# Fewer adaLN pieces at the output projection and the router, more inside the mixer and in attention's softmax loop

## The chip, the cores and the metric

One Trainium2 chip, one core of it. The metric is the device time of one launch in microseconds (us), lower is better. TensorE is called PE here, VectorE DVE, ScalarE ACT, GpSimd POOL and SyncE SP; SP issues nearly all transfers.

## The reference, cut to what matters

Two networks run one behind the other on 256 tokens of width 1024. The first has two layers, each a mixer and then sixteen experts:

```python
for layer in range(DEPTH):            # DEPTH = 2
    h = h + hybrid_mixer(rms_norm(h, norm1_g[layer]), w_in[layer], ..., w_out[layer], lb)
    h = h + expert_choice_ffn(rms_norm(h, norm2_g[layer]), w_router[layer], w_gate[layer],
                              w_up[layer], w_down[layer])
```

The second network has two layers too: pooling with an MLP, then attention with an MLP. Each modulates its inputs with six vectors, which come from a small conditioning vector through a large matrix, for the latent rows (`c`) and the context rows (`c_ctx`):

```python
sh1, sc1, gt1, sh2, sc2, gt2 = split(silu(c) @ w_ada[i] + b_ada[i])     # w_ada[i]: 1024 x 6144
h_lat = modulate(rms_norm_2(x, g_mix_pre[i]), sh1, sc1)
x = x + gt1 * rms_norm_2(mixer(h_lat), g_mix_post[i])
x = x + gt2 * rms_norm_2(mlp(modulate(rms_norm_2(x, g_mlp_pre[i]), sh2, sc2)), g_mlp_post[i])
```

All of it is float32. The 24 pieces `w_ada[i][:, 512 n : 512 n + 512]` depend on nothing else in the computation, so each may be loaded and multiplied wherever the kernel has room before its vector is wanted. A piece is written (layer, n) below; (1, 10) and (1, 11) make `gt2` of the second layer, wanted only by the last MLP.

## The kernel before, in words

The work is laid out by hand, one program for each engine. All weights pass through a ring of slots of 2 MB: seven fixed ones, and up to four more while the experts run (two in `ring_extra`, one each in `ring_late` and `ring_early`), which lie in memory that the mixer uses until its last matmuls. `items` gives every load its slot and its place in one order of use. The counter `weights_used` rises by one for each used item; a load waits until it has passed the value stored in `free_at`. SP issues loads strictly in the order of its own program, so a load whose slot isn't free holds back all behind it.

**A mixer** (layers 0 and 1 of the first network) runs nine projections. The last four (RV, HI, RG, HG) go by rows: for each of two row tiles t, `project_rows` does 24 matmuls (L567 to L569, three for each of eight chunks, since each product is split into high and low parts), then `one_level` does one level of a scan (L723; DVE prepares it). Behind some of these eight steps, those in `EARLY_AFTER`, `early_ada` puts one ada piece: first the columns of the piece before (`ada_columns`, L595), then the product (`ada_item`, L580), whose row ACT copies out (`ada_row`). All early pieces share one ring slot, called d, so each is loaded only when the one before has been used. Behind them come the scan's outputs (`hgrn_out`, L753 and L755). SP waits for these before it loads anything into `ring_extra`.

**Output projection and router.** `rest_ada(0)` and `rest_ada(1)` lie between the parts of the output projection (`w_out`), `rest_ada(2)` before the second tile's logits, and `rest_ada(3)` behind the turned affinities, all in slots b and d. Then tokens are gathered (L902) and the experts begin; SP loads their weights as slots come free.

**Attention** takes 16 steps u (`scores` L1399, softmax on DVE and ACT, `turn_probs` L1408, `values` L1420 every second step), then the product with `w_o` (L1449). Two more pieces follow it. `ADA_LAST` names the pieces that are done in the second network; their slot is ring slot 6. POOL makes a diagonal of `gt2` and PE turns it into rows (`post_rows`, L1201).

Of the kernel before, what the change touches and what calls it, by code (L numbers as in the profile page):

```python
# [87 lines left out]

EARLY_AFTER = ((RV, 0), (RV, 1), (HI, 1), (RG, 0), (HG, 0), (HG, 1))


def pieces(layer, first, end):
    return [(layer, n) for n in range(first, end)]


ADA_EARLY = (pieces(0, 0, 6), pieces(0, 10, 12) + pieces(1, 0, 4))
ADA_REST = (pieces(0, 6, 10), pieces(1, 4, 6) + pieces(1, 10, 12))
ADA_LAST = pieces(1, 8, 10) + pieces(1, 6, 8)  # L100


GROUP = 4
# [21 lines left out]
def build_program(nc, x, cols, w_in, w_out, w_router, w_gate, w_up, w_down, final_g, ctx_x, w_ada,  # L125
# [221 lines left out]
    for layer in range(DEPTH):  # L347
        rounded_free.append(count[2][4:6])
        a, b, c, d = sorted(range(4), key=lambda slot: count[2][slot])
        early = iter(ADA_EARLY[layer])  # L350
        for n, kind in enumerate(PROJECTIONS):
            if (kind, 0) in EARLY_AFTER:
                item(("ada", *next(early)), d, 1)
            item(("mix", layer, n), (a, b, c, d, a, b, c, a, b)[n], 1)
            if (kind, 1) in EARLY_AFTER:
                item(("ada", *next(early)), d, 1)
        for piece, slot in zip(ADA_REST[layer], (b, d)):
            item(("ada", *piece), slot, 1)
        rounded = [4 + (SPLITS * layer + j) % 2 for j in (OUT_0, OUT_1)]
        own = RING1 - 1  # L360
        for n in range(2):
            item(("w_out", layer, n), (c, a)[n], 1)
            count[2][rounded[n]] = count[0]
        for piece, slot in zip(ADA_REST[layer][2:], (b, d)):
            item(("ada", *piece), slot, 1)
        slots = itertools.chain((rounded[0], c, RING1, RING1 + 1, own, EARLY, a, b, d, rounded[1],
                                 LATE),
                                itertools.cycle((c, rounded[0], own, a, b, d, rounded[1])))
        for e in range(NEXP):
            for n in (0, 2):  # L370
                for part, slot in enumerate(sorted(itertools.islice(slots, 2))):
                    item(("moe", layer, e, n + part), slot, 2 if (e, n) == (0, 0) else 1)
            for n in (4, 5):
                item(("moe", layer, e, n), next(slots), 1)
            if e in CTX_MID[layer]:
                item(("ctx", CTX_MID[layer][e]), next(slots), 1)
# [6 lines left out]
    ring2, last_pieces = itertools.cycle(order2), [("ada", *piece) for piece in ADA_LAST]  # L383
    for layer in range(DEPTH):
        item(last_pieces[layer], RING1 - 1 if layer else next(ring2), 1)
        for name in block2_first(layer):
            item(name, next(ring2), 1)
        if layer:
            item(last_pieces[2], RING1 - 1, 1)
            item(last_pieces[3], next(ring2), 1)  # L390
        for n in range(16):
            item(("mlp", layer, n), next(ring2), 1)
# [136 lines left out]
    def _(pe):  # L529
# [73 lines left out]
        for l in range(DEPTH):  # L603
# [172 lines left out]
            def rest_ada(k):  # L776
                ada_item(ADA_REST[l][k], 2)

# [52 lines left out]
            def logits(t):  # L831
# [6 lines left out]
                for c in range(KC):  # L838
# [7 lines left out]
            out_0 = len(PROJECTIONS)  # L846
            rows_times(take(pe, names[0], 0), 0, out_0, 1, chunks=first)
            turn_mixed(1, lambda t: freed(pe, ("hgrn_o", l, t)))
            rest_ada(0)
            rows_times(take(pe, names[1], 1), 1, out_0, None, chunks=first)  # L850
            fill(rows_times(psum[0], 0, out_0, 1, chunks=second), names[0])
            rest_columns(0)
            rest_ada(1)
            fill_and_release(rows_times(psum[1], 1, out_0, None, chunks=second), names[1],
                             ("w_out", l, 0))
            rest_columns(1)
            for t in range(NT):
                name = ("w_out", l, 1, t)
                ins = rows_times(take(pe, name, t), t, out_0 + 1, None, amid if t else {})
# [3 lines left out]
                    fill(ins, name)  # L863

            turn_rows(1)
            rest_ada(2)
            logits(1)
            rest_columns(2)
            pe.wait_ge(S_("affinity_ready"), NT * (l + 1))
            name = ("affT", l)  # L870
            ps = take(pe, name, 5)
            for t in range(NT):
                ins = turn(ps[0:NEXP, t * P:(t + 1) * P], aff[:, t, :], ident)
            fill(ins, name)
            rest_ada(3)
            rest_columns(3)

            def spread_out(part):

# [508 lines left out]

        for pair in range(2):
            turn_queries(pair, 2 + pair)  # L1390
        for pair in range(2):
            freed(pe, ("qT", pair))
        freed(pe, "kT")
# [31 lines left out]
        for u in range(NQ * NT):  # L1425
            if u == 1:
                for pair in (2, 3):
                    turn_queries(pair, 2 + pair)
            if u + 2 == NQ:
                for pair in (2, 3):  # L1430
                    freed(pe, ("qT", pair))
            if u + 2 < NQ * NT:
                scores(u + 2)
            if u and u % 2 == 0:
                values(u // 2 - 1)
            turn_probs(u)
        values(NQ - 1)
        freed(pe, ("o", NQ - 4))
        freed(pe, ("o", NQ - 3))
# [26 lines left out]
    def _(act):  # L1466
# [89 lines left out]
        for l in range(DEPTH):  # L1556
# [102 lines left out]
                  scale=1.0 / W4).then_inc(S_("std_ready"), 1)  # L1659
            high_item(l, OUT_1)  # L1660
            high_chunks(("mix", l), mix_gain, (2, 3))
            for k in range(2):
                ada_row(ADA_REST[l][k])


            def out_ready(t):
                for n in range(2):
# [15 lines left out]
                           lambda _, t=t: xs[:, t, :], first=t)  # L1683
                odd_rows(t)
            step(f(spare[:, :], eps[:, :], ACT.Exp))
            ada_row(ADA_REST[l][2])
            for t in range(NT):
                expect("router_max_ready")
                name = ("logit", l, t)
                ps = full(act, name)  # L1690
                free(f(logit[:, t, :], ps[:, 0:NEXP], ACT.Exp, scale=rinv[:, t:t + 1],
                       bias=rstats[:, t, 1:2], accum_out=rstats[:, t, 2:3]), name)
            ada_row(ADA_REST[l][3])

            def ctx_stats(src):

# [258 lines left out]

        for pair in range(2):
            query_copies(pair)

        def exponentials(u):
            expect("score_max_ready")  # L1960
# [6 lines left out]
        for u in range(NQ * NT):  # L1967
            if u + 1 < NQ * NT:
                exponentials(u + 1)
            if u == 1:  # L1970
                for pair in (2, 3):
                    query_copies(pair)
            name = ("pT", u)
            ps = full(act, name)
            t = u % NT
            free(f(prT[:, :, t * P:(t + 1) * P], ps[:, :].rearrange("p (a t) -> p a t", a=4),
                   ACT.Copy), name)
        first_high(1)
        for t in range(NT):
            bank_stats(t, [("wo", n, t) for n in range(2)])  # L1980
# [13 lines left out]
    def _(dve):  # L1994
# [110 lines left out]
        for l in range(DEPTH):  # L2105
# [267 lines left out]
                    free(tt(h[:, t, part], h[:, t, part], ps[:, :], ALU.add), name)  # L2373

            gains(l, 0, "g_mix_pre")
            ada_bias(("rest", l), ADA_REST[l])
            if l == 0:
                gains(0, 1, "g_mlp_pre")

            def ctx_normalise():  # L2380
# [369 lines left out]
        score_max(0)  # L2750
        score_max(1)
        gains(1, 1, "g_mlp_pre")
        for u in range(NQ * NT):
            freed(dve, ("s", u))
            step(reciprocal(soft[:, u % 4, 3:4], soft[:, u % 4, 2:3]))
            ts(pr[:, u % 2, :], pr[:, u % 2, :], soft[:, u % 4, 3:4], None,
               ALU.mult).then_inc(S_("prob_ready"), 1)
            if u + 2 < NQ * NT:
                score_max(u + 2)
            if u >= 2 and u % 2 == 0:  # L2760
                take_values(u // 2 - 1)
        take_values(NQ - 1)
        first_low(1)
        for t in range(NT):
# [14 lines left out]
    def _(pool):  # L2779
# [62 lines left out]
        diagonal(0, 1, 0, "g_mlp_post")  # L2842
        split_odd_banks("xm0")
        clear_sums(NT, X4_BEFORE["mlp0"])
        freed(pool, ("rest", 1))
        full(pool, ("rows_mlp0", 0, 1))
        diagonal(1, 0, 0, "g_mix_post")
        full(pool, ("rows_mix1", 0, 1))
        diagonal(1, 1, 0, "g_mlp_post")
        split_odd_banks("xm1")  # L2850
        clear_sums(NT, X4_BEFORE["mlp1"])
# [3 lines left out]
    def _(sp):  # L2855
# [20 lines left out]
        for l in range(DEPTH):  # L2876
# [30 lines left out]
            def load_expert(e, n):  # L2907
# [5 lines left out]
                else:  # L2913
# [3 lines left out]

            names = ([("mix", l, n) for n in range(len(PROJECTIONS))] + [("moe", l, FIRST_OWN)]
                     + [("w_out", l, n) for n in range(2)] 
                     + [("ada", *piece) for piece in ADA_EARLY[l] + ADA_REST[l][0:2]])  # L2920
            def turn_of(name):

                name = ("moe", l, 0, name[2]) if name[0] == "moe" else name
# [47 lines left out]
            for e in range(NEXP):  # L2971
                for n in (2, 3, 0, 1, 4, 5) if e == 0 else range(6):
                    if (e, n) == (1, 2):
                        full(sp, ("logit", l, NT - 1))
                        load_expert(1, 4)
                    if (e, n) == (2, 1):
                        ctx_rows_and_bands()
                    if (e, n) not in ((0, FIRST_OWN), (0, 5), (1, 3), (1, 4)):
                        load_expert(e, n)
                    if (e, n) == (0, 3):  # L2980
                        freed(sp, ("hgrn_o", l, NT - 1))
                        sp.dma_start(wr[:, :, :], w_router[l].rearrange("(p c) e -> p c e", c=KC)
                                     ).then_inc(S_("router_landed"), 16)
                        load_expert(0, 5)
                        for piece in ADA_REST[l][2:]:
                            early(("ada", *piece))
                    if (e, n) == (0, 1):
                        load_expert(1, 3)
                if e in CTX_MID[l]:
                    load_ctx(CTX_MID[l][e])  # L2990
        for l in range(DEPTH):
# [10 lines left out]
                else:  # L3002
                    load(name, chunked(w_o[:, (n - 3) * 512:(n - 2) * 512]), eight)

            names = block2_first(l) + (last_pieces[1:] if l else last_pieces[:1])
            if l == 0:
                sp.wait_ge(S_("ctx_x_ready"), 2 * NT)
                full(sp, (("cxa", 1), 3))
# [13 lines left out]
                             src.rearrange("(c p) n -> p c n", p=P)).then_inc(landed[slot], 16)  # L3022

            for n in range(4):
                sp.wait_ge(weights_used, free_at[("mlp", l, n)])
                mlp_load(n, w_mlp_in[l, :, n % 2 * 512:(n % 2 + 1) * 512],
                         w_mlp_out[l, n % 2 * 512:(n % 2 + 1) * 512, :])
# [111 lines left out]
```

## Time and profile before

| | |
|---|---|
| median of 3 runs | 1953.57 us (1952.56 to 1953.98) |
| the profiled execution | 1954.41 us, its span in the profile 1952.6 us |
| busy: PE / DVE / ACT / POOL | 87% / 41% / 27% / 2% of the span |
| moved | 626.57 MB, 321 GB/s on average |
| chain that ended last | PE 58%, DMA 32%, ACT 4%, DVE 4% |

The stages, from the profile's slices and windows: mixer 0 to about 168 us; output projection, router and experts of layer 0 to about 700 us; mixer 1 to about 872 us; the experts of layer 1 to about 1406 us; pooling and the first MLP to about 1629 us; attention to about 1755 us; the last MLP to the end. From 60 to 168 us the 16 DMA engines are busy 0.63 of the time and PE 104.92 of 108 us. In the table of windows below, the DMA share can read slightly over 1, since busy times are rounded for each packet. A duration on PE holds the tail of the pipeline, so the distance from one row's start to the next is what an operation takes from PE's time.

### The profile page before, as it was taken

The page shows a single profiled execution, that of the slowest core. Times are in us where ns is not written, and L with a number is a line of the kernel's source. Part 1 is how long each engine was busy: PE and PEld are TensorE (multiplying, and loading weights), DVE is VectorE, ACT ScalarE, POOL GpSimd, SP SyncE. Part 2 cuts the span into 40 slices and gives each one's busy share as a digit, 9 for nine tenths or more (in the row PEclk, how much of TensorE's full clock was granted, in tenths as well). Part 3 has the DMA queues.
Part 4 walks back from the last instruction along what each step waited for, and adds up shares of the span by engine and source line. Part 5 has one row for each costly group of instructions (what it writes and reads, how often), then busy time and mean ns, then how long its engine had stood idle before and what let it go on. Part 6 is the DMA issues. An engine that isn't in the chain of part 4 may idle for free.

```text
span 1952.6 us, 26219 instructions
## 1 busy us (share of the span) xinstructions
PE 1696.5 (87%) x10892; PEld 1125.2 (58%) x10892; DVE 791.1 (41%) x1203; ACT 526.9 (27%) x802; POOL 30.0 (2%) x27
## 2 busy tenths in 40 slices
PE   7999877689888679998868887977789999999998
PEld 6877433245344249776343543522279985448897
DVE  6595312101111044975101111120077676647776
ACT  5633222100000037342100000021164343444342
POOL 0000000000000000000000000000030000000000
PEclk9999889889989989998989989979799999999999
DMA  9478999999999995679999999999955464315451
GB/s 358 162 269 335 425 430 421 427 422 423 420 427 421 426 385 182 242 265 419 427 423 423 423 424 421 426 428 423 416 190 196 172 233 154 129 49 208 175 182 55
DMA packets 125511, 626.57 MB, mean 321 GB/s; under 512 B 5091, under 2 KB 7779, under 8 KB 100198
## 3 DMA queue, kind: packets, MB, share of 16 engines
q1 hardware_dynamic: 124978, 624.85, 79.5%
q8 instruction: 73, 1.20, 0.2%
q10 hardware_dynamic: 436, 0.32, 0.1%
q14 instruction: 24, 0.20, 0.0%
HBM read 622.01 MB, written 3.15 MB: 320 GB/s over the span
## 4 chain that ended last, share of the span: by engine, by line
PE 58%; DMA 32%; ACT 4%; DVE 4%; issue 1%; SPq 0%; POOL 0%; DVEq 0%; ACTq 0%
DMA ring<-in_w_up 15%; PE bank L567 9%; PE bank L569 9%; PE bank L568 9%; DMA ring<-in_w_mlp_in 8%; DMA ring<-in_w_mlp_out 6%; PE bank L1086 6%; PE bank L1104 5%; PE bank L947 5%; PE bank L1332 2%; PE bank L580 2%; PE bank L1449 1%; DMA ring<-in_w_down 1%; PE bank L982 1%; PE bank L723 1%; DMA ring<-in_w_ada 1%
## 5 line engine op out<-in xcount | busy, mean ns | idle before, releaser
L947 PE MATMUL bank<-ring,xeT 128*32 128x512 f32 x1920 | 266.4, 702 | 98.2 <-DMA ring<-in_w_up 97.8
L947 PEld LDWEIGHTS bank<-ring,xeT 128*32 128x32 f32 x1920 | 68.6, 121 | 283.5 <-issue 283.0
L475 ACT ACTIVATE silu_g<-bank 128x256 f32<-128x256 f32 x32 | 12.3, 383 | 690.1 <-PE bank L947 690.1
L475 DVE TENSOR_TENSOR hid_e<-silu_g,bank 128x256 f32<-128x256 f32 x32 | 13.5, 421 | 374.0 <-ACT silu_g L475 374.0
L2567 DVE TENSOR_TENSOR w_low<-ring,w_high 128x1024 fp32r<-128x1024 f32 x128 | 152.4, 1233 | 10.2 <-ACT w_high L1858 5.3
L1858 ACT ACTIVATE w_high<-ring 128x1024 fp32r<-128x1024 f32 x128 | 126.5, 1050 | 85.0 <-PE bank L569 85.0
L1086 PE MATMUL bank<-ctx_xT,ring 128*128 128x256 f32 x512 | 125.3, 410 | 26.1 <-DMA ring<-in_w_mlp_in 26.1
L567 PE MATMUL bank<-x_high,w_high 128*128 128x256 f32 x512 | 145.1, 283 | 3.0 <-DVE x_low L475 2.4
L982 PE MATMUL bank<-ring,hid_T 128*32 128x256 f32 x1920 | 120.5, 397 | 30.9 <-DMA ring<-in_w_down 23.6
L568 PE MATMUL bank<-x_low,w_high 128*128 128x256 f32 x512 | 144.8, 283 | 0.0
L569 PE MATMUL bank<-x_high,w_low 128*128 128x256 f32 x512 | 144.7, 283 | 0.0
L1104 PE MATMUL bank<-ring,ctx_hid 128*128 128x512 f32 x256 | 126.1, 655 | 21.2 <-DMA ring<-in_w_mlp_out 21.2
L1086 PEld LDWEIGHTS bank<-ctx_xT,ring 128*128 128x128 f32 x512 | 105.6, 208 | 46.9 <-DMA ring<-in_w_mlp_in 30.4
L567 PE MATMUL bank<-w_high,xs_high 128*128 128x512 f32 x256 | 105.0, 410 | 5.8 <-DVE xT_low L475 4.9
L475 DVE TENSOR_TENSOR w_low<-ring,w_high 128x2048 fp32r<-128x2048 f32 x44 | 100.9, 2293 | 18.8 <-ACT w_high L475 14.6
L1104 PEld LDWEIGHTS bank<-ring,ctx_hid 128*128 128x128 f32 x256 | 53.2, 211 | 92.1 <-issue 66.2
L982 PEld LDWEIGHTS bank<-ring,hid_T 128*32 128x32 f32 x1920 | 59.3, 112 | 81.5 <-DMA ring<-in_w_down 32.6
L569 PE MATMUL bank<-w_high,xT_low 128*128 128x512 f32 x256 | 102.3, 400 | 0.0
L568 PE MATMUL bank<-w_low,xs_high 128*128 128x512 f32 x256 | 102.2, 399 | 0.0
L567 PE MATMUL bank<-w_high,hid_high 128*128 128x512 f32 x256 | 101.0, 395 | 0.0
L569 PE MATMUL bank<-w_high,hid_low 128*128 128x512 f32 x256 | 101.0, 394 | 0.0
L568 PE MATMUL bank<-w_low,hid_high 128*128 128x512 f32 x256 | 100.9, 394 | 0.0
(282 smaller groups left out, 2595.9 us busy)
## 6 DMA issues: line engine op xcount, KB each, us to landing
ring<-in_w_down SPq DMA_DIRECT2D x60, 2048.0 KB, 30.2
ring<-in_w_up SPq DMA_DIRECT2D x60, 2048.0 KB, 24.3
ring<-in_w_gate SPq DMA_DIRECT2D x60, 2048.0 KB, 21.8
ring<-in_w_ada SPq DMA_DIRECT2D x24, 2048.0 KB, 9.6
ring<-in_w_mlp_in SPq DMA_DIRECT2D x24, 2048.0 KB, 8.4
ring<-in_w_mlp_out SPq DMA_DIRECT2D x24, 2048.0 KB, 7.9
ring<-in_w_in SPq DMA_DIRECT2D x16, 2048.0 KB, 9.2
ring<-in_w_out SPq DMA_DIRECT2D x4, 2048.0 KB, 7.8
```

The source lines that it names most:

```text
L475: self.ins, self.mine = op(*args, **kw), "none"
L567: mm(ps, lh, rh, start=first, stop=False, skip_group_check=True)
L568: mm(ps, lh, rl, start=False, stop=False, skip_group_check=True)
L569: return mm(ps, ll, rh, start=False, stop=last, skip_group_check=True)
L580: ins = mm(ps[32 * g:32 * g + 32, :], cT[:, 2 * g + k, :], w[:, 2 * g + k, :], start=k == 0, stop=k == 1)
L947: ins = mm(ps[32 * j:32 * j + 32, :], xeT[:, g % 2, c, i * CAP:(i + 1) * CAP], w[:, :, k, j, :, :], start=c == 0, stop=c == KC - 1, skip_g ...
L982: ins = mm(banks[q // 2][rows_, at_:at_ + 256], hidT[:, j, 32 * block:32 * block + 32], w[:, c, 256 * q:256 * (q + 1)], start=(n, c) == (0 ...
L1086: ins = mm(ps[:, (j % 2) * S:(j % 2 + 1) * S], w[:, c, j * P:(j + 1) * P], cxT[:, c, :], start=c == 0, stop=c == KC - 1)
L1104: ins = mm(ps[:, :], chid[:, c, t * P:(t + 1) * P], w[:, c, half * 512:(half + 1) * 512], start=c == 0, stop=c == 3)
L1332: ins = mm(ps[:, :], xT2[:, c, t * P:(t + 1) * P], w[:, c, :], start=c == 0, stop=c == KC - 1)
L1858: raw(w_high[:, n % 2, quarter(q)], ring[:, slot, quarter(q)], ACT.Copy).then_inc(S_("w_high_ready"), 1)
L2567: nc.vector.tensor_tensor(w_low[:, slot, quarter(q)], ring[:, slot, quarter(q)], w_high[:, n % 2, quarter(q)].bitcast(F32), ALU.subtract). ...
```

## The change

Two of layer 0's ada pieces, (0, 6) and (0, 7), and two that ran in layer 1, (1, 4) and (1, 5), move from between the parts of the output projection into the mixer's two free steps, behind (HI, 0) and (RG, 1). Each mixer has eight early pieces then, one behind every step. Layer 0 keeps two pieces around its router. Layer 1 keeps none there: its (1, 10) and (1, 11) move to attention, where the first is multiplied behind the turning of the first queries and the second between the last two `turn_probs`. Their rows become columns in the first step and behind the last one.

```diff
-EARLY_AFTER = ((RV, 0), (RV, 1), (HI, 1), (RG, 0), (HG, 0), (HG, 1))
+EARLY_AFTER = tuple((kind, t) for kind in (RV, HI, RG, HG) for t in range(2))
...
-ADA_EARLY = (pieces(0, 0, 6), pieces(0, 10, 12) + pieces(1, 0, 4))
-ADA_REST = (pieces(0, 6, 10), pieces(1, 4, 6) + pieces(1, 10, 12))
-ADA_LAST = pieces(1, 8, 10) + pieces(1, 6, 8)
+ADA_EARLY = (pieces(0, 0, 8), pieces(0, 10, 12) + pieces(1, 0, 6))
+ADA_REST = (pieces(0, 8, 10), [])
+ADA_LAST = pieces(1, 8, 10) + pieces(1, 6, 8) + pieces(1, 10, 12)
...
             turn_mixed(1, lambda t: freed(pe, ("hgrn_o", l, t)))
-            rest_ada(0)
             rows_times(take(pe, names[1], 1), 1, out_0, None, chunks=first)
             fill(rows_times(psum[0], 0, out_0, 1, chunks=second), names[0])
-            rest_columns(0)
-            rest_ada(1)
             fill_and_release(rows_times(psum[1], 1, out_0, None, chunks=second), names[1],
                              ("w_out", l, 0))
-            rest_columns(1)
...
             turn_rows(1)
-            rest_ada(2)
+            if ADA_REST[l]:
+                rest_ada(0)
             logits(1)
...
         for pair in range(2):
             turn_queries(pair, 2 + pair)
+        ada_item(ADA_LAST[4], 6)
...
             if u + 2 < NQ * NT:
                 scores(u + 2)
+            if u == 0:
+                last_columns(4, 7)
             if u and u % 2 == 0:
                 values(u // 2 - 1)
             turn_probs(u)
+            if u == NQ * NT - 2:
+                ada_item(ADA_LAST[5], 0)
+        last_columns(5, 1)
         values(NQ - 1)
```

ACT gets the two `ada_row` copies at the same places, and DVE `last_bias(4)` ahead of the loop and `last_bias(5)` behind it. POOL waits for both before the diagonal for the last MLP, where it waited for layer 1's rest before. SP loads both pieces into slot 6, and the piece (1, 6) of `ADA_LAST`, which needs the same slot, behind them, between the first two loads of the last MLP.

## Rows read from the trace of the kernel before

**Rows 1.** Windows: length, busy us of each engine, granted clock, DMA share, GB/s

```profile
168.00:690.00 522.00, 420.35 (x2911) 221.09 (x2910) 89.50 (x161) 57.49 (x106) 2.10 (x2) 0.91 1.01 424
872.00:1400.00 528.00, 427.58 (x2906) 219.90 (x2910) 89.66 (x162) 63.75 (x117) 4.20 (x4) 0.91 1.01 424
```

**Rows 2.** Timeline of PE and one DVE row in the mixers: start, length, operation

```profile
97.57 1.95 PE L723 MATMUL bank<-qdec,kdec 128*128 128x128 f32 x16
99.35 0.95 PE L595 MATMUL bank<-consts_sb,ada_rows 128*128 128x2 f32 x8
100.24 1.92 PE L580 MATMUL bank<-ring,silu_c 128*32 128x512 f32 x16
102.09 0.50 PE L567 MATMUL bank<-w_high,xs_high 128*128 128x512 f32 x1
...
107.77 1.95 PE L723 MATMUL bank<-qdec_even,kdec 128*128 128x128 f32 x16
...
129.28 1.92 PE L580 MATMUL bank<-ring,silu_c 128*32 128x512 f32 x16 [1.22 <-DMA ring<-in_w_ada]
...
832.71 1.93 PE L580 MATMUL bank<-ring,silu_c 128*32 128x512 f32 x16 [1.64 <-DMA ring<-in_w_ada]
...
101.99 1.23 DVE L475 TENSOR_TENSOR qdec_even<-hgrn_q,hgrn_f 128x1024 f32<-128x1024 f32 x1
```

**Rows 3.** Timeline of SP: issues in mixer 0 and at its end

```profile
97.76 0.37 SPq L2865 DMA_DIRECT2D ring<-in_w_in  x1
102.22 0.37 SPq L2865 DMA_DIRECT2D ring<-in_w_ada  x1
...
168.05 0.34 SPq L2865 DMA_DIRECT2D ring_extra<-in_w_gate  x1
```

**Rows 4.** DMA issues, mixers: us to landing of those at 102.22, 131, 805.23

```profile
ring<-in_w_ada SPq DMA_DIRECT2D x1, 2048.0 KB, 9.7
...
ring<-in_w_ada SPq DMA_DIRECT2D x1, 2048.0 KB, 7.9
...
ring<-in_w_ada SPq DMA_DIRECT2D x1, 2048.0 KB, 9.9
```

**Rows 5.** DMA issues, the same columns: those at 168.05, 871.52, 903.94, 929.09

```profile
ring_extra<-in_w_gate SPq DMA_DIRECT2D x1, 2048.0 KB, 9.8
...
ring_extra<-in_w_gate SPq DMA_DIRECT2D x1, 2048.0 KB, 9.2
...
ring<-in_w_up SPq DMA_DIRECT2D x1, 2048.0 KB, 12.3
...
ring<-in_w_down SPq DMA_DIRECT2D x1, 2048.0 KB, 11.7
```

**Rows 6.** Timeline of layer 1's router: PE, and two issues of SP

```profile
903.94 0.33 SPq L2865 DMA_DIRECT2D ring<-in_w_up  x1
...
907.95 1.93 PE L839 MATMUL bank<-router_sb,xT 128*128 128x16 f32 x16 [0.25 <-issue]
...
929.09 0.33 SPq L2865 DMA_DIRECT2D ring<-in_w_down  x1
```

**Rows 7.** Timeline of attention's loop, its first and last steps

```profile
1681.00 4.51 PE L1399 MATMUL bank<-kT,qT 128*128 128x512 f32 x6 [2.29 <-ACT qT L475]
...
1685.21 0.37 DVE L475 SCALAR_TENSOR_TENSOR mod_gain<-mods,cols_sb 128x8 f32<-128x8 f32 x2
...
1685.69 0.16 DVE L475 RECIPROCAL softmax_stat<-softmax_stat 128x1 f32<-128x1 f32 x1
...
1720.87 0.60 PE L1408 MATMUL bank<-consts_sb,prob 128*128 128x128 f32 x4
...
1722.34 0.66 PE L1408 MATMUL bank<-consts_sb,prob 128*128 128x128 f32 x4 [0.87 <-DVE prob L475]
...
1723.73 1.10 PE L1420 MATMUL bank<-probT,kv 128*128 128x256 f32 x4 [0.73 <-issue]
```

**Rows 8.** The diagonal for the last MLP: POOL makes it, PE needs it

```profile
1636.72 1.90 POOL L475 TENSOR_TENSOR diag<-consts_sb,gate_col 128x1024 f32<-128x1024 f32 x1
...
1739.26 1.88 PE L1201 MATMUL bank<-diag,ones 128*128 128x512 f32 x4
```

More of the change, by code:

```diff
@@ L356, in build_program @@
                 item(("ada", *next(early)), d, 1)
-        for piece, slot in zip(ADA_REST[layer], (b, d)):
-            item(("ada", *piece), slot, 1)
         rounded = [4 + (SPLITS * layer + j) % 2 for j in (OUT_0, OUT_1)]
@@ L363, in build_program @@
             count[2][rounded[n]] = count[0]
-        for piece, slot in zip(ADA_REST[layer][2:], (b, d)):
+        for piece, slot in zip(ADA_REST[layer], (b, d)):
             item(("ada", *piece), slot, 1)
@@ L385, in build_program @@
         item(last_pieces[layer], RING1 - 1 if layer else next(ring2), 1)
-        for name in block2_first(layer):
+        for k, name in enumerate(block2_first(layer)):
+            if k == 3:
+                item(last_pieces[4], RING1 - 1, 1)
+                item(last_pieces[5], RING1 - 1, 1)
             item(name, next(ring2), 1)
@@ L865, in _ @@
             turn_rows(1)
-            rest_ada(2)
+            if ADA_REST[l]:
+                rest_ada(0)
             logits(1)
-            rest_columns(2)
+            if ADA_REST[l]:
+                rest_columns(0)
             pe.wait_ge(S_("affinity_ready"), NT * (l + 1))
@@ L874, in _ @@
             fill(ins, name)
-            rest_ada(3)
-            rest_columns(3)
+            if ADA_REST[l]:
+                rest_ada(1)
+                rest_columns(1)
             def spread_out(part):
@@ L1661, in _ @@
             high_chunks(("mix", l), mix_gain, (2, 3))
-            for k in range(2):
-                ada_row(ADA_REST[l][k])
             def out_ready(t):
@@ L1685, in _ @@
             step(f(spare[:, :], eps[:, :], ACT.Exp))
-            ada_row(ADA_REST[l][2])
+            if ADA_REST[l]:
+                ada_row(ADA_REST[l][0])
             for t in range(NT):
@@ L1692, in _ @@
                        bias=rstats[:, t, 1:2], accum_out=rstats[:, t, 2:3]), name)
-            ada_row(ADA_REST[l][3])
+            if ADA_REST[l]:
+                ada_row(ADA_REST[l][1])
             def ctx_stats(src):
@@ L1957, in _ @@
             query_copies(pair)
+        ada_row(ADA_LAST[4])
         def exponentials(u):
@@ L1977, in _ @@
                    ACT.Copy), name)
+            if u == NQ * NT - 2:
+                ada_row(ADA_LAST[5])
         first_high(1)
@@ L2375, in _ @@
             gains(l, 0, "g_mix_pre")
-            ada_bias(("rest", l), ADA_REST[l])
             if l == 0:
+                ada_bias(("rest", l), ADA_REST[l])
                 gains(0, 1, "g_mlp_pre")
@@ L2752, in _ @@
         gains(1, 1, "g_mlp_pre")
+        last_bias(4)
         for u in range(NQ * NT):
@@ L2761, in _ @@
                 take_values(u // 2 - 1)
+        last_bias(5)
         take_values(NQ - 1)
@@ L2844, in _ @@
         clear_sums(NT, X4_BEFORE["mlp0"])
-        freed(pool, ("rest", 1))
         full(pool, ("rows_mlp0", 0, 1))
@@ L2848, in _ @@
         full(pool, ("rows_mix1", 0, 1))
+        freed(pool, ("last", 4))
+        freed(pool, ("last", 5))
         diagonal(1, 1, 0, "g_mlp_post")
@@ L2919, in _ @@
                      + [("w_out", l, n) for n in range(2)]
-                     + [("ada", *piece) for piece in ADA_EARLY[l] + ADA_REST[l][0:2]])
+                     + [("ada", *piece) for piece in ADA_EARLY[l]])
             def turn_of(name):
@@ L2984, in _ @@
                         load_expert(0, 5)
-                        for piece in ADA_REST[l][2:]:
+                        for piece in ADA_REST[l]:
                             early(("ada", *piece))
@@ L3003, in block2_load @@
                     load(name, chunked(w_o[:, (n - 3) * 512:(n - 2) * 512]), eight)
-            names = block2_first(l) + (last_pieces[1:] if l else last_pieces[:1])
+            names = block2_first(l) + (last_pieces[1:2] + last_pieces[3:] if l else last_pieces[:1])
             if l == 0:
@@ L3024, in _ @@
             for n in range(4):
+                if (l, n) == (1, 1):
+                    block2_load(last_pieces[2])
                 sp.wait_ge(weights_used, free_at[("mlp", l, n)])
```

## The prediction, made before the changed kernel was run

> **What bounds the kernel now.** I read the chain that ended last, then the stages in windows, then the timelines of PE and SP around each edit, and last the time that single loads take to land. In both stages of experts the DMA engines are busy all the time at 424 GB/s, while PE is busy for about 0.8 of it [rows 1]. There only two things count: when this stream of loads starts, and how many bytes are in it. The stream starts when the mixer's last matmuls free `ring_extra` [rows 3]. So the end of the mixer on PE sets the start of the next five hundred microseconds. Inside the mixer PE runs without a gap: level, columns, ada product and projection follow each other start to start [rows 2]. DVE had the level that starts on PE at 107.77 ready at 103.22 (101.99 plus 1.23), so it isn't what PE waits for. The only gaps in these steps are those where an ada load is late, 1.22 us in mixer 0 and 1.64 us in mixer 1.
>
> **Work added to the mixers.** A step takes from PE, start to start: level 1.78 (97.57 to 99.35), columns 0.89 (to 100.24), ada product 1.85 (to 102.09), projection 5.68 (to 107.77). A piece more costs 1.85 + 0.89 = 2.7 us, two pieces 5.5 us in each mixer, on the path. The copies of their rows on ACT lie beside PE's next projection.
>
> **Loads that come late.** All eight pieces share slot d. A piece is issued 0.13 us after the one before was used (102.22 against 102.09 [rows 2, 3]) and is wanted one projection, one level and one set of columns later: 5.68 + 1.78 + 0.89 = 8.35, less 0.13, which leaves 8.2 us. Alone, a load lands after 7.9 us, in time by 0.3. Behind another load, issued 4.46 us earlier (97.76 and 102.22), it lands after 9.7 us in mixer 0 and 9.9 us in mixer 1 [rows 4], 1.5 and 1.7 us too late. A projection's weights are issued behind every second row tile, so every second early piece has such a companion. Before, most pieces had a free step ahead of them in which the load could land; the one without it is the 1.22 and 1.64 us gap. After the change two further pieces stand so: the one behind (HI, 0), whose load is the very one issued at 102.22, and the one behind (HG, 0). I take 1.5 + 1.3 us in mixer 0 and 1.7 + 1.6 us in mixer 1. Those behind (HI, 1) and (RG, 1) load alone and cost nothing, at most 1.2 each if they collide after all. The one behind (HG, 1) has the retention output ahead of it. The mixers end later by x = 5.5 + 2.8 = 8.3 us and 5.5 + 3.3 = 8.8 us; with no late load x would be 5.5.
>
> A rule to weigh here. The Trainium skill (DMA: Bandwidth & Descriptors, Anatomy of one DMA) fits a transfer, issued from GpSimd, as about 2.0 us fixed plus its bytes at 436 GB/s. By that estimate a piece of 2 MB lands after 6.8 us, and one that follows a companion by 4.46 us after 7.2 us, so no load would be late and the first rival below would hold. The trace has 7.9 and 9.7 us, from SP [rows 4].
>
> **What layer 0 makes of it.** Before, the DMA engines were still moving the two pieces for the output projection when `ring_extra` came free: its first load took 9.8 us to land [rows 5]. After, these two went earlier, the engines stand idle, and that load takes the 7.9 us of a lone one. Its issue is 8.3 us later, its landing 8.3 - 1.9 = 6.4 us. The stream behind it holds the same bytes as before. The output projection gives PE its 5.5 us back, but that is no help: PE is then 2.8 us late in front of a stream that is 6.4 us late. The two pieces left at this router sit where they sat. Layer 0: +6.4 us. Bounds: +3.6 with no late load, +8.8 if two more loads are late.
>
> **What layer 1 makes of it.** Here two pieces leave the stream, 4.2 MB at 424 GB/s, 9.9 us. Its start is later by 8.8 - 1.3 = 7.5 (the first load took 9.2 [rows 5]), so by bytes alone the stream would end 2.4 us earlier. But loads also need free slots. With the pieces out of the output projection PE ends it 8.8 - 5.5 = 3.3 us late; the load that this frees, at 903.94, landed 12.3 us after its issue and can do it in 7.9: 3.3 - 4.4 = -1.1 us. Then every slot is full until the first expert's first matmuls; the load that they free at 929.09 landed after 11.7 us, at best 7.9: 3.3 - 3.8 = -0.5 us [rows 5, 6]. The latest of the three rules: -0.5 us. The stream is shorter by nearly 10 us, but it runs dry in front of the router and hardly gains. Taking the pieces out of the router's waits gives nothing: the logits start 0.25 us after PE was free [rows 6], held by ACT's and DVE's copies, and PE idles behind them. A gain of up to 0.5 us from ACT's missing copies is possible.
>
> **What attention makes of it.** The first product (1.85 us) fits into the 2.29 us in which PE waits for ACT's copies of the queries [rows 7]. Its columns come behind the scores of step 2, which end at 1685.51, and DVE's bias waits for them in front of the first reciprocal, at 1685.69. Last case: 1685.51 + 0.89, then the bias, about 0.2: 1.0 us late. Best case: the filled gap makes scores end sooner, and only the bias counts, 0.2. I take 0.6. The second product starts at 1721.47 and ends at 1723.3, where the last `turn_probs` started at 1722.34: 1.0 us late. The columns then take 0.89 us of a gap of 0.73 that the copy left before `values` [rows 7], about 0.3 with the wait for the row's own copy. Attention: +1.9 us, bounds 1.0 and 2.8. Two things queue behind new waits without cost. SP now holds the last MLP's first load until the first of the two pieces is used, at about 1681, and its other loads follow in time, since ACT asks for that MLP's first weights only behind the loop. POOL's diagonal now starts behind the loop, at about 1725, takes 1.90 us and a short product, and PE wants it at 1739.26 [rows 8]. If this cover of some ten microseconds were gone, its whole length would be on the path.
>
> **Sum.** With x the same in both mixers: layer 0 gives x - 1.9, layer 1 gives x - 9.3 (5.5 + 3.8), attention 1.9, together 2x - 9.3. With 8.3 and 8.8: 6.4 - 0.5 + 1.9 = +7.8 us. On the profiled execution's own 1954.41 that is 1962.2; on the median of 1953.57, which is 0.84 below it, 1961.4 us.
>
> **Rivals.** *No load is late.* x = 5.5, the sum is +1.7 us, 1955.3 us. For it: the two loads that would be late are judged by single rows. Against: one of them is the same load at the same distance from its companion. Chance 0.17.
>
> *The moved work is hidden, and the shorter stream counts: faster.* If the mixer's steps are really paced by DVE, whose levels take nearly as long as PE's steps, more work on PE lengthens nothing. x = 0, 2x - 9.3 is -9.3 us, 1944.3 us. It ends faster wherever x stays below 4.7 us. Against: PE has no gap in a step with an ada piece, and DVE is ahead by 4.5 us [rows 2]. Chance 0.08.
>
> *Every new load is late.* The pieces behind (HI, 1) and (RG, 1) had 0.3 us to spare; shifted steps may bring them beside a projection's load, 1.2 us each. x rises by 2.4, the sum by 4.8: +12.6 us, 1966.2 us. Chance 0.15.
>
> **How the numbers follow.** My own case has 0.60 and a range of 1957.8 to 1964.5 (bounds of attention, 0.5 at the router, 1 us in each x). The range over all leaves out the fast rival and the far end of the last one: 1953.5 to 1966. A difference below 0.2%, 3.9 us, can't be told from none here. My case and the last rival are slower, 0.73 with a little of my case's low end taken off; the first rival is the same, 0.18; the fast one 0.09.
>
> **What would show it.** In the timeline of PE, a wait for `in_w_ada` of 1 to 2 us at three early pieces in each mixer instead of one; `hgrn_out` about 8 us later in mixer 0; the first `ring_extra` load landing in about 8 us with idle DMA engines ahead of it; the experts of layer 0 ending 6 us later, those of layer 1 taking, from the end of layer 0 to their own end, the time that they took, with a dip of the DMA share near the router; and the last `turn_probs` a microsecond late behind an ada product. The prediction is wrong if the mixers grow by less than 5 us, or if a mixer's lateness shrinks within the stage of experts behind it.

## The result, and the profile after

The changed kernel takes 1975.14 us (median of 4, 1973.14 to 1977.99) where the kernel before, run beside it, takes 1953.28 (median of 4). The ratio is 1.0108, 95% interval 1.0095 to 1.012. That is slower, as forecast, but by 21.9 us instead of 7.8, and outside the range. The profiled execution took 1973.14 us, with a span of 1971.4: 18.8 us over the span of before.

Where the two spans part, in us from the start (each mark is the start of a row in the timelines; "+" is after less before):

| mark | before | after | + | forecast |
|---|---|---|---|---|
| mixer 0 over: first `ring_extra` load issued | 168.05 | 183.59 | 15.5 | 8.3 |
| layer 1 begins (ACT scales `h`) | 709.79 | 721.90 | 12.1 | 6.4 |
| mixer 1 over | 871.52 | 895.99 | 24.5 | 15.2 |
| second network begins | 1418.71 | 1435.41 | 16.7 | 5.9 |
| attention's first scores | 1681.00 | 1697.91 | 16.9 | 5.9 |
| first product with `w_o` | 1725.53 | 1744.70 | 19.2 | 7.8 |
| end | 1952.6 | 1971.4 | 18.8 | 7.8 |

The mixers hold the miss: 15.5 and 12.4 us against 8.3 and 8.8. PE's timeline of the changed kernel has every ada product of mixer 0, and behind "..." those of mixer 1 that waited (line numbers are one higher than before):

```profile
90.85 1.92 PE L581 MATMUL bank<-ring,silu_c 128*32 128x512 f32 x16
101.04 1.92 PE L581 MATMUL bank<-ring,silu_c 128*32 128x512 f32 x16
112.96 3.50 PE L581 MATMUL bank<-ring,silu_c 128*32 128x512 f32 x16 [1.65 <-DMA ring<-in_w_ada]
124.75 1.92 PE L581 MATMUL bank<-ring,silu_c 128*32 128x512 f32 x16
137.14 3.36 PE L581 MATMUL bank<-ring,silu_c 128*32 128x512 f32 x16 [2.13 <-DMA ring<-in_w_ada]
148.78 1.92 PE L581 MATMUL bank<-ring,silu_c 128*32 128x512 f32 x16
160.82 3.47 PE L581 MATMUL bank<-ring,silu_c 128*32 128x512 f32 x16 [1.77 <-DMA ring<-in_w_ada]
176.13 1.92 PE L581 MATMUL bank<-ring,silu_c 128*32 128x512 f32 x16
...
827.19 1.92 PE L581 MATMUL bank<-ring,silu_c 128*32 128x512 f32 x16 [1.68 <-DMA ring<-in_w_ada]
...
849.48 3.13 PE L581 MATMUL bank<-ring,silu_c 128*32 128x512 f32 x16 [1.82 <-DMA ring<-in_w_ada]
...
873.15 2.91 PE L581 MATMUL bank<-ring,silu_c 128*32 128x512 f32 x16 [1.58 <-DMA ring<-in_w_ada]
```

Three waits in each mixer, at the three places named. Before, the one product that waited ran in 1.92 us all the same [rows 2]. Here five of six take 2.9 to 3.5 us. The windows over a product in time and over the three slow ones of mixer 0 say why (the columns are those of [rows 1]; the third number from the end is the granted clock, its share of 2.4 GHz):

```profile
112.90:116.30 3.40, 3.34 (x16) 0.60 (x16) 3.13 (x5) 0.00 (x0) 0.00 (x0) 0.52 0.00 0
124.70:126.60 1.90, 1.90 (x18) 0.45 (x17) 1.80 (x4) 0.00 (x0) 0.00 (x0) 1.00 1.01 393
137.10:140.40 3.30, 3.26 (x16) 0.59 (x16) 3.16 (x3) 0.00 (x0) 0.00 (x0) 0.55 0.00 0
160.80:164.20 3.40, 3.38 (x16) 0.60 (x16) 2.92 (x2) 0.00 (x0) 0.00 (x0) 0.53 0.00 0
```

Behind the wait PE runs at 1.2 GHz, and the same sixteen matmuls take almost twice as long. The Trainium skill (TensorE: Matmul & The Clock Gate, HAM oscillation) describes a kernel in which a wait for DMA before each short piece of matmul work makes the clock fall again and again. This trace agrees that waits for DMA bring the clock down, with 3.36 to 3.50 us behind the waits of mixer 0 and 1.92 elsewhere. But the waits in the Trainium skill's example are about 3 to 5 us long and its pieces of work about 2 us, while here waits of 1.65 to 2.13 us do it, with over 20 us of work between them.

The half clock could have been seen in the trace of the kernel before. Six matmuls behind a wait of 2.29 us took 4.51 us in [rows 7], where the changed kernel has 2.81 for them, and the second ada product at layer 1's router already ran at a granted clock of 0.50:

```profile
912.57 3.64 PE L580 MATMUL bank<-ring,silu_c 128*32 128x512 f32 x16
```

The landings of the three loads behind a companion, issued at 103.03, 126.73 and 150.76, and then those of the first `ring_extra` load of each layer and of the load that the first expert frees, at 951.04:

```profile
ring<-in_w_ada SPq DMA_DIRECT2D x1, 2048.0 KB, 9.9
ring<-in_w_ada SPq DMA_DIRECT2D x1, 2048.0 KB, 10.4
ring<-in_w_ada SPq DMA_DIRECT2D x1, 2048.0 KB, 10.0
...
ring_extra<-in_w_gate SPq DMA_DIRECT2D x1, 2048.0 KB, 7.4
...
ring_extra<-in_w_gate SPq DMA_DIRECT2D x1, 2048.0 KB, 7.3
...
ring<-in_w_down SPq DMA_DIRECT2D x1, 2048.0 KB, 7.4
```

They answer to [rows 4, 5]: the late ones land 0.2 to 0.7 us later than the 9.7 us of the load issued at 102.22, the others even earlier than the 7.9 us of the forecast. The router of layer 1 without its two pieces, and attention's loop, against [rows 6, 7]:

```profile
921.42 1.92 PE L840 MATMUL bank<-router_sb,xT 128*128 128x16 f32 x16
...
928.53 3.57 PE L840 MATMUL bank<-router_sb,xT 128*128 128x16 f32 x16 [1.71 <-DVE xT L476]
...
942.81 2.47 PE L902 MATMUL bank<-onehot,xs 128*128 128x128 f32 x10 [1.03 <-DVE onehot L476]
...
1697.91 2.81 PE L1400 MATMUL bank<-kT,qT 128*128 128x512 f32 x6 [0.44 <-issue]
1700.56 0.95 PE L596 MATMUL bank<-consts_sb,ada_rows 128*128 128x2 f32 x8
...
1739.34 1.92 PE L581 MATMUL bank<-ring,silu_c 128*32 128x512 f32 x16
1741.19 0.66 PE L1409 MATMUL bank<-consts_sb,prob 128*128 128x128 f32 x4
...
1742.89 1.11 PE L1421 MATMUL bank<-probT,kv 128*128 128x256 f32 x4
1743.75 1.90 POOL L476 TENSOR_TENSOR diag<-consts_sb,gate_col 128x1024 f32<-128x1024 f32 x1
```

The second logits took 1.93 us before and take 3.57 now. From the first logits to the gather it is 21.39 us now and was 19.57 (901.18 to 920.75). The first scores of attention went the other way: 2.81 us instead of 4.51. POOL's diagonal is over at 1745.65, 12.8 us before PE wants it.

### The profile page after: what moved, and what is told of

It reads as the page before. It is cut to its first block, busy times and chain, and to the rows that moved or that the text cites. A ratio compares the mean times of both kernels' runs of the same rounds, so it can differ in the third digit from the quotient of the medians.

```text
span 1971.4 us, 26225 instructions
## 1 busy us (share of the span) xinstructions
PE 1702.6 (86%) x10892; PEld 1129.2 (57%) x10892; DVE 790.8 (40%) x1203; ACT 527.2 (27%) x802; POOL 29.1 (1%) x27
## 4 chain that ended last, share of the span: by engine, by line
PE 56%; DMA 33%; ACT 5%; DVE 4%; issue 1%; SPq 0%; POOL 0%; DVEq 0%; ACTq 0%
DMA ring<-in_w_up 15%; DMA ring<-in_w_mlp_in 9%; PE bank L568 9%; PE bank L570 9%; PE bank L569 9%; PE bank L1086 7%; DMA ring<-in_w_mlp_out 6%; PE bank L947 5%; PE bank L1104 5%; DMA ring<-in_w_ada 3%; PE bank L581 2%; PE bank L1332 2%; PE bank L1455 1%; PE bank L982 1%; ACT w_high L476 1%; DVE w_low L476 1%
## 5 line engine op out<-in xcount | busy, mean ns | idle before, releaser
L1104 PE MATMUL bank<-ring,ctx_hid 128*128 128x512 f32 x256 | 119.8, 628 | 22.6 <-DMA ring<-in_w_mlp_out 22.6
L476 DVE TENSOR_TENSOR w_low<-ring,w_high 128x2048 fp32r<-128x2048 f32 x44 | 100.9, 2293 | 21.9 <-ACT w_high L476 17.9
```

The lines of the kernel that those rows point to most:

```text
L476: self.ins, self.mine = op(*args, **kw), "none"
L1104: ins = mm(ps[:, :], chid[:, c, t * P:(t + 1) * P], w[:, c, half * 512:(half + 1) * 512], start=c == 0, stop=c == 3)
```

## The experiments

**Is it the late loads?** The three early pieces behind a companion load only two of their eight chunks; the products run in full over what lies in the slot, so the kernel leaves out part of the data and computes something else.

```diff
+                elif what == "ada" and (owner, n) in [ADA_EARLY[l][k] for k in (2, 4, 6)]:
+                    load(name, [src[0:2 * P, :].rearrange("(c p) n -> p c n", p=P)], ...)
                 else:
                     load(name, chunked(src), eight)
```

> The changed kernel, but the ada loads for the pieces behind (HI, 0), (RG, 0) and (HG, 0) move only two of their eight chunks, in both layers; their products run in full, on what lies in the slot. Theory (a late load costs its wait and then a product at half the clock): the three waits for in_w_ada go, those products take 1.9 us again, hgrn_out is about 10 us earlier in mixer 0 and 7 us in mixer 1 than in the changed kernel; of that about 10 and 5 us reach the end (layer 1 is then held by the release of slots): about 1960 us, 15 less than the changed kernel. Rival (the extra ada work itself, or DVE's pace, makes the mixers longer): still 1970 to 1975 us.

Measured: 1953.96 us (10 runs), 1.0002 of before (0.9993 to 1.0012), span 1952.8. No ada product in the mixers waits and each takes 1.92 or 1.93 us. So the late loads with all that follows from them are the whole of what is measured, 21 us (this run also moves fewer bytes; the order of loads below takes 15 of the 21 away with all bytes moved). The pieces in the mixers, without lateness, cost nothing in the end: the mixers take 5.2 and 4.0 us longer than before, the stages of experts behind them 4.4 and 6.4 less (537.3 and 540.8 us), attention's loop 1.5 more. The prediction's sum for this case, its first rival, was 1955.3 us. Start to start, from the first ada product to the last, mixer 0 has these rows in the kernel before, with six products:

```profile
90.04 1.92 PE L580 MATMUL bank<-ring,silu_c 128*32 128x512 f32 x16
...
160.61 1.92 PE L580 MATMUL bank<-ring,silu_c 128*32 128x512 f32 x16
```

and these here, with eight:

```profile
90.86 1.92 PE L581 MATMUL bank<-ring,silu_c 128*32 128x512 f32 x16
101.05 1.92 PE L581 MATMUL bank<-ring,silu_c 128*32 128x512 f32 x16
...
165.82 1.92 PE L581 MATMUL bank<-ring,silu_c 128*32 128x512 f32 x16
```

That is 70.57, 74.96, and 85.28 us (90.85 to 176.13) in the changed kernel: late loads cost 10.32 us of mixer 0. An ordinary step takes 10.19 to 10.20 us. The steps of the changed kernel that end in a wait take 1.72, 2.19 and 1.84 us more (5.75), those that begin with a slow product 1.59, 1.44 and 1.54 more (4.57): together 10.32. In mixer 1 it is 8.54: 5.29 of lateness and 3.25 of half clock.

**Is the clock part of it?** The loads stay late, but PE works while it would wait.

```diff
+            if filler:
+                ps = take(pe, ("row", *piece), bank)
+                for _ in range(filler):
+                    mm(ps[:, :], xs_high[:, 0, 0, :], xs_high[:, 0, 0:4, :], start=True, stop=True)
             w = wait_landed(pe, tag)...
...
-                ada_item(ADA_EARLY[l][k], 6)
+                ada_item(ADA_EARLY[l][k], 6, 7 if k in (2, 4, 6) else 0)
```

> The changed kernel, all loads in full, but PE runs 7 matmuls of 128x512 (about 1.6 us, their result is overwritten) ahead of each of the three late pieces, in place of idling. Theory that the idle wait lowers the granted clock: the products behind it take 1.9 us and not 2.9 to 3.5; about 4.7 us less in mixer 0 and 2.2 us in mixer 1, 1968 us. Rival (the slow product has another cause, or the clock falls at random): the products stay slow and the time stays at 1975 us or above.

Measured: 1966.0 us (4 runs), 1.0067 (1.0051 to 1.0084). Nine us go by adding work of no use.

```profile
110.52 1.86 PE L578 MATMUL bank<-xs_high 128*128 128x512 f32 x7
112.31 1.92 PE L587 MATMUL bank<-ring,silu_c 128*32 128x512 f32 x16
```

No product is slow, and next to no wait is left behind the filler: a late step now costs about what the filler takes, 1.71 to 1.95 us. Mixer 0 takes 80.21 us from first to last ada product, 5.07 less than the changed kernel's 85.28.

**How long may a wait be?** Seven chunks of eight, and three matmuls of filler instead of seven.

```diff
-                    load(name, [src[0:2 * P, :]...
+                    load(name, [src[0:7 * P, :]...
```

```diff
-                ada_item(ADA_EARLY[l][k], 6, 7 if k in (2, 4, 6) else 0)
+                ada_item(ADA_EARLY[l][k], 6, 3 if k in (2, 4, 6) else 0)
```

> The changed kernel, but the three early pieces behind a companion load seven of their eight chunks of weights (it leaves out the loading of the eighth; the products run over what lies in the slot). Question: does the price of a late load grow with its lateness, or does the second half of it (the product at half clock) fall away at once? 256 KB less at the 424 GB/s of a busy stream is 0.6 us, so the waits of 1.65, 2.13 and 1.77 us shrink to about 1.0, 1.5 and 1.1. Theory 1 (a step: a short wait leaves the granted clock up, since waits of 0.98 to 1.22 us had 1.92 us products behind them): at least two of the three products in mixer 0 take 1.92 us instead of 3.4 to 3.5, mixer 0 ends about 5 us earlier than in the changed kernel (at about 178.5 instead of 183.59), and the time is about 1966, 8 to 10 below it. Theory 2 (the price is proportional, or the clock falls for another reason than the wait): the products stay at 3.0 to 3.5 us, mixer 0 ends 1.8 us earlier, and the time is about 1971.

> The changed kernel, with three instead of seven matmuls of 128x512 in the row's own bank ahead of each of the three late early pieces: 0.8 us of work at full pace (seven took 1.80 us), so that about 0.9 to 1.3 us of waiting is left behind them. The loads are whole and land as late as before. Theory 1 (the length of the idle time decides on the clock): the products behind take 1.92 us as with seven, each late step costs the lateness of the load alone (1.7 to 2.1 us), and the time is that of seven matmuls, 1966, plus or minus 1. Theory 2 (only a full cover keeps the clock): products of 3.0 us or more at two or three of the places, and 1970 to 1975.

Seven chunks: 1961.86 us (5 runs), 1.0048 (1.0029 to 1.0066). All the products run in 1.92 us, and an eighth less to load saves 13 of 22 us, more than expected. The waits also shrank more than expected, to 0.88 to 1.07 us (1.0, 1.5 and 1.1 were forecast for mixer 0), so this run doesn't tell what a wait of 1.5 us would have done.

```profile
112.46 1.92 PE L581 MATMUL bank<-ring,silu_c 128*32 128x512 f32 x16 [0.98 <-DMA ring<-in_w_ada]
...
133.87 1.92 PE L581 MATMUL bank<-ring,silu_c 128*32 128x512 f32 x16 [0.95 <-DMA ring<-in_w_ada]
...
155.34 1.92 PE L581 MATMUL bank<-ring,silu_c 128*32 128x512 f32 x16 [0.99 <-DMA ring<-in_w_ada]
```

Short filler: 1969.18 us (4 runs, 1965.02 to 1972.01), 1.0069 (1.005 to 1.0088), three above the forecast 1966; the ratio is that of seven matmuls. The profiled execution is the slowest of the four. In mixer 1 its three waits are 0.77 to 0.95 us, with full-speed products. In mixer 0 two loads landed after 11.3 and 11.4 us instead of some 10:

```profile
113.06 1.92 PE L587 MATMUL bank<-ring,silu_c 128*32 128x512 f32 x16 [0.91 <-DMA ring<-in_w_ada]
...
136.61 3.55 PE L587 MATMUL bank<-ring,silu_c 128*32 128x512 f32 x16 [2.29 <-DMA ring<-in_w_ada]
...
161.87 1.92 PE L587 MATMUL bank<-ring,silu_c 128*32 128x512 f32 x16 [2.36 <-DMA ring<-in_w_ada]
```

The longest wait of all has a full-speed product behind it. So the length of the wait does not decide alone, and theory 1 is only half right: the short waits did no harm, and what decides behind the longer ones stays open.

**Can the order of the loads cure it?** SP issues each early piece ahead of its companion, not behind it.

```diff
+            order = sorted(names, key=turn_of)
+            for companion, k in ((("mix", l, 8), 2), (("w_out", l, 0), 4), (("w_out", l, 1), 6)):
+                order.remove(companion)
+                order.insert(order.index(("ada", *ADA_EARLY[l][k])) + 1, companion)
+            for name in order:
```

> The changed kernel with its whole computation; SP only issues the three companions (HG's weights and both output projection loads) behind the ada load that they delayed instead of ahead of it. Theory (a late load and the clock behind it are the loss): the three waits go in both mixers, hgrn_out comes where it came with the short loads (173 and 876 us), about 1954 us, no difference to before. Rival (the short loads helped by moving fewer bytes, not by being in time): waits stay, above 1965 us.

Measured: 1959.98 us (7 runs), 1.0028 (1.0017 to 1.0039). 15 us better than the change, but 6 worse than expected: a miss. The companion takes 14.1 us to land and reaches into the next piece's load, which I had counted as alone. Here are the landings of the piece that SP issued at 103.28 and of the companion that it issued at 103.70, and what PE made of it:

```profile
ring<-in_w_ada SPq DMA_DIRECT2D x1, 2048.0 KB, 9.2
ring<-in_w_in SPq DMA_DIRECT2D x1, 2048.0 KB, 14.1
```

```profile
112.55 1.92 PE L581 MATMUL bank<-ring,silu_c 128*32 128x512 f32 x16 [0.98 <-DMA ring<-in_w_ada]
123.20 1.92 PE L581 MATMUL bank<-ring,silu_c 128*32 128x512 f32 x16 [0.39 <-DMA ring<-in_w_ada]
134.46 1.92 PE L581 MATMUL bank<-ring,silu_c 128*32 128x512 f32 x16 [0.99 <-DMA ring<-in_w_ada]
```

Five waits of 0.38 to 1.00 us in mixer 0, with a full-speed product behind each. That isn't safe in every execution: the kernel of the next run has the same mixers and the same order, and in its trace one wait in mixer 0 (at 133.75) is 1.32 us long and the product behind it takes 3.62 us. Mixer 0 takes 79.05 us, 4.1 over the run without late loads, mixer 1 76.51, 1.6 over it: together 5.7 of the six.

**What does the empty router cost?** The kernel of the run above, with four useless matmuls of 128x512 of float32 ahead of layer 1's second logits.

```diff
+            else:
+                ps = take(pe, ("filler", l), 2, readers=0)
+                for _ in range(4):
+                    mm(ps[:, :], ones[:, :], ident_all[:, 0:512], start=True, stop=True)
             logits(1)
```

> The changed kernel with the ada loads first, and four matmuls of 128x512 at the place in layer 1's router that the moved piece left, their result unused. Theory (without the piece PE idles there, its clock falls and the second tile's logits take 3.6 instead of 1.9 us): logits 1.9 us again, the gather of layer 1 about 1.6 us nearer to the end of the mixer, 1 to 1.6 us less than with the ada loads first alone. Rival (ACT and DVE hold the router anyway): no difference.

Measured: 1961.73 us (5 runs), 1.0037 (1.0023 to 1.0051), no gain: a miss. The second logits run in 1.85 us instead of 3.56, but the filler takes 4.25, its end holds them up, and the gather starts 21.72 us behind the first logits, as against 21.48 without it. So a filler of this length can't tell what the clock is worth here; the attention-only run below does.

**The two halves of the change.** Attention's part alone, on the kernel before (the two pieces leave layer 1's router), and the mixers' part alone, on the changed kernel (they stay there). Only the lists are shown; the calls at their places move with them.

```diff
-ADA_REST = (pieces(0, 6, 10), pieces(1, 4, 6) + pieces(1, 10, 12))
-ADA_LAST = pieces(1, 8, 10) + pieces(1, 6, 8)
+ADA_REST = (pieces(0, 6, 10), pieces(1, 4, 6))
+ADA_LAST = pieces(1, 8, 10) + pieces(1, 6, 8) + pieces(1, 10, 12)
```

```diff
-ADA_REST = (pieces(0, 8, 10), [])
-ADA_LAST = pieces(1, 8, 10) + pieces(1, 6, 8) + pieces(1, 10, 12)
+ADA_REST = (pieces(0, 8, 10), pieces(1, 10, 12))
+ADA_LAST = pieces(1, 8, 10) + pieces(1, 6, 8)
```

> The kernel before with only pieces (1, 10) and (1, 11) moved to attention. Theory (a shorter stream is held by the release of slots ahead of the router, and the router's logits run at half the clock without the ada products): mixers as before, the experts of layer 1 end only 2 to 3 us earlier, attention costs 2.2 us: 1952 to 1954 us, no difference to before. Rival (bytes count): 9.9 us less in layer 1, 1945.5 us.

> The changed kernel, but pieces (1, 10) and (1, 11) stay around layer 1's router. Theory: mixer 0 and layer 0 as in the changed kernel (+12 us), layer 1 +10 us, attention 0: 1975 to 1977 us, all of the loss comes from the mixers. Rival (attention or the shortened router is part of the loss): below 1970 us.

Attention alone: 1953.19 us (10 runs), 0.9994 (0.9984 to 1.0004). Mixers alone: 1975.66 (4 runs), 1.0113 (1.0096 to 1.013). All of the loss is in the mixers' half; the attention half is worth nothing that can be measured. Its loop takes 46.8 us in this run and in the changed kernel, against 44.5 before; in the other runs that have it, 46.0 to 48.1.

At the router, the second logits of the attention-only run and of the last run of this document, which has the same operations there:

```profile
906.32 1.93 PE L842 MATMUL bank<-router_sb,xT 128*128 128x16 f32 x16 [2.09 <-DVE xT L478]
...
903.62 3.57 PE L842 MATMUL bank<-router_sb,xT 128*128 128x16 f32 x16 [2.10 <-DVE xT L478]
```

First logits to gather take 19.41 us in the first and 21.06 in the second. With the pieces kept they take 19.57 before and 19.78 in the mixers-only run. So leaving PE idle there costs nothing as such; it costs 1.6 to 2.1 us more than these 19.41 when the clock falls, as it does in seven of the eight traces without pieces and without filler there (21.06 to 21.48 us). And the pieces don't protect for certain: the kernel before with its order cured, below, keeps them, and its stretch takes 20.68 us, with an ada product of 2.65.

**A version from what was learnt.** Only the one late load of the kernel before is cured, by the order of two issues; then the same with attention's half.

```diff
+            order = sorted(names, key=turn_of)
+            for companion, k in ((("w_out", l, 0), 3),):
+                order.remove(companion)
+                order.insert(order.index(("ada", *ADA_EARLY[l][k])) + 1, companion)
+            for name in order:
```

> The kernel before, with the first output projection load issued behind the ada load that it delayed. Theory: the one wait in each mixer (1.2 and 1.6 us) goes and nothing takes its place; both experts' stages start that much earlier and the end comes 2.9 us earlier, 1950.9 us. Rival (the wait was covered): 1953.8 us.

> The kernel before with both: the order of the last run, and only (1, 10) and (1, 11) moved to attention. Theory: the two effects add, 2.9 us and the 0.6 us that the move alone gave: 1950.3 us, faster than both kernels. Rival (bytes count once nothing is late): below 1947 us.

Measured: 1949.81 us (11 runs), 0.998 (0.9971 to 0.9989), and 1949.88 (11 runs), 0.9976 (0.9967 to 0.9985). Both beat both kernels, by 4 us and by 25, and both come within 1.1 us of what was expected. Attention's half adds nothing to the order. No ada product waits. The companion takes 14.2 us here as well, but a free step lies in front of the next piece. First to last ada product is 69.28 us in both mixers, against 70.57 and 71.03 before.

## Why the prediction was wrong

**Work added.** Right. Without any wait, eight products take 74.96 us from first to last and six take 69.28: 5.7 us, where 5.5 were forecast.

**Loads that come late.** This step failed: it priced a late load at its lateness alone. The places were right (three a mixer, those behind (HI, 0) and (HG, 0) new), and that (HI, 1) and (RG, 1) load in time too. The price was not. Forecast, with the late load of before, 1.22 + 2.8 = 4.0 us in mixer 0 and 1.64 + 3.3 = 4.9 in mixer 1; measured 10.32 and 8.54. Of the difference, 4.57 + 3.25 us is half clock behind the waits, which the sum had no term for: [rows 2] showed two products at 1.92 and 1.93 us behind waits of 1.22 and 1.64, and I took that for the rule, though [rows 7] had the 4.51 us row behind a wait. The rest is the lateness itself: 5.75 us instead of 4.0 in mixer 0, where the loads landed after 9.9 to 10.4 us, and 5.29 instead of 4.9 in mixer 1. Another 0.8 us is that the first ada product of mixer 0 already starts 0.8 us later, which it also does in kernels that are no slower.

**Layer 0.** Forecast x - 1.9, measured x - 3.4: the idle DMA engines in front of `ring_extra` were seen (busy 0.24 of the time in the 15.5 us ahead of its first load, against 0.82 in the 16 us ahead of it before), and the lone load lands sooner than thought. The expectation that a mixer's lateness stays through the experts held; what was given back beyond 1.9 is within what this stage varies by (541.7 us before, 539.4 in the attention run, whose layer 0 is the same). Over all traces the stage takes 537.3 to 538.9 us with the changed mixers and 539.4 to 541.7 without.

**Layer 1.** Forecast x - 9.3, measured 12.4 - 7.8: 1.5 us less came back. PE got back 4.2 of the 5.5 us in the output projection (from the end of the mixer to the first logits 25.43 us instead of 29.66). "Taking the pieces out of the router's waits gives nothing" holds where the clock stays up, as the attention-only run shows; in the profiled execution it fell, and first logits to gather took 1.8 us more. The dip of the DMA share near the router is there, 0.73 from 920 to 930 us and 0.83 from 950 to 960.

**Attention.** Forecast +1.9, bounds 1.0 to 2.8; measured +2.3 in the loop. The second product starts at 1739.34, and the last `turn_probs` follows right behind it at 1741.19. The diagonal was hidden, as said.

**Sum.** In spans 15.5 - 3.4 + 12.4 - 7.8 + 2.3 - 0.2 = 18.8, against 7.8. The mixers are 7.2 and 3.6 of the 11.0 missed, and the layers' 1.5 less and 1.5 more cancel. The median lies 3 us further off, as the profiled execution was the fastest of the four and that of before 1.1 us above its median.

## What to carry to other kernels

A late load costs more than its lateness where PE has nothing else to do: find the wait, and look at the duration of the row behind it. A single row at full speed behind a wait is no proof of the opposite. No wait for an ada load of up to 1.11 us cost the clock here, whether it was an eighth less to load, an earlier issue or useless matmuls that had made it short; one of 1.32 us did. Before more pieces are put through one slot, compare the time between a slot's release and its next use with the landing behind a companion, not with the landing alone; and when two loads go out together, put the one that is wanted first in front, if a free step lies behind it.

## What the runs showed of the hardware

- In the mixers of all traces, all 25 waits for an ada load of up to 1.11 us (short filler 4, seven chunks 6, the order alone on the changed kernel 8, the same with the router's filler 6, attention alone 1) have a product of 1.92 or 1.93 us behind them. Of the 18 from 1.22 to 2.36 us (kernel before 2, changed kernel 6, mixers alone 6, short filler 2, attention alone 1, router's filler 1), ten have one of 2.5 to 3.6. What decides between them these runs don't tell: 1.64, 1.68 and 2.36 us were harmless, 1.32, 1.54 and 1.58 once each were not.
- The same operations behind the same idle time can run at either clock: sixteen matmuls of the router took 1.93 us behind 2.09 us of waiting in one run and 3.57 behind 2.10 in another.
- A load of 2 MB issued 4.46 us behind a companion lands after 9.4 to 11.4 us in different executions and places.
- Of two loads of 2 MB issued 0.4 us apart, in five pairs of two runs, the first lands after 7.9 to 9.2 us and the second after 12.9 to 14.2. With 9.2 and 14.1 the second is not through when the next load is issued, 11.2 us after the first.
- Two ada pieces more cost PE 5.7 us in a mixer (74.96 us against 69.28), and two less give back 4.2 us in the output projection.
